# A transformer trunk on one core: the last expert round of each layer in smaller pieces, and what follows it begun on parts

## The reference, cut to what matters

```
for layer in range(2):
    x = x + mixer(rmsnorm(x, norm_mix[layer]))      # layer 0: attention, layer 1: gated linear attention
    x = x + moe(rmsnorm(x, norm_ffn[layer]))        # 32 experts, two of one group for each token
return rmsnorm(x, norm_final)

# moe, for each expert e
hid = silu(h @ w_gate[e]) * (h @ w_up[e])           # 1024 -> 512
y = y + gates[..., e:e + 1] * (hid @ w_down[e])     # 512 -> 1024
```

## Time and profile before

| | us |
|---|---|
| median of three runs | 1184.77 |
| lowest and highest | 1184.62, 1185.75 |
| span of the profiled execution | 1184.7 |
| PE busy in it | 998.1 (84%) |
| DVE, ACT, POOL busy | 276.8, 130.1, 3.5 |

### The profile page before, as it was taken

The page is one execution under the profiler, slowest core; times in us unless marked ns, Lnnn a source line. Parts: engine busy times, 40 slices in busy tenths (PEclk is TensorE's granted clock), DMA queues, the critical chain, the costliest instruction groups (busy, mean ns, idle before and its releaser), DMA issues.

```text
span 1184.7 us, 12720 instructions
## 1 busy us (share of the span) xinstructions
PE 998.1 (84%) x5268; PEld 457.9 (39%) x5268; DVE 276.8 (23%) x653; ACT 130.1 (11%) x309; POOL 3.5 (0%) x10
## 2 busy tenths in 40 slices
PE   8999999967767768977999999999677777779776
PEld 7675553313213213342485555533132132233422
DVE  1265352202102101110322453512011011012103
ACT  2024020000000000000231120200000000000001
POOL 0000000000000000000000000000000000000000
PEclk9999999989879879988999999999898798799889
DMA  9923989999999999999973518999999999999996
GB/s 365 411 77 133 418 329 425 428 427 428 427 430 427 428 429 427 426 426 423 412 327 142 213 71 340 352 428 426 426 430 427 428 429 426 429 427 428 425 422 249
DMA packets 39297, 442.43 MB, mean 373 GB/s; under 512 B 4386, under 2 KB 4770, under 8 KB 12484
## 3 DMA queue, kind: packets, MB, share of 16 engines
q1 hardware_dynamic: 39092, 441.47, 89.4%
q10 hardware_dynamic: 144, 0.13, 0.0%
HBM read 440.54 MB, written 1.05 MB: 373 GB/s over the span
## 4 chain that ended last, share of the span: by engine, by line
PE 52%; DMA 42%; issue 3%; DVE 1%; SPq 1%; ACT 0%; POOL 0%; DVEq 0%; POOLq 0%
PE psum L1707 51%; DMA sb_weights<-moe_w_down 38%; DMA sb_weights<-moe_w_gate 3%; SPq L668 1%; DMA sb_weights<-moe_w_up 1%; DMA sb_weights<-ev_w_in_units 1%; PE psum L2302 0%; DVE sb_weights L1578 0%; DVE sb_x L1598 0%; PE psum L1885 0%; PE psum L1745 0%; PE psum L2170 0%; PE psum L2080 0%; PE psum L1983 0%; ACT sb_weights L914 0%
## 5 line engine op out<-in xcount | busy, mean ns | idle before, releaser
L1707 PE MATMUL psum<-sb_weights,sb_hT 128*32 128x512 f32 (+3 forms) x2368 | 469.4, 629 | 102.9 <-DMA sb_weights<-moe_w_gate 59.8
L1707 PE MATMUL psum<-sb_weights 128*32 128x512 f32 (+12 forms) x1632 | 319.8, 561 | 43.5 <-DMA sb_weights<-moe_w_down 38.7
L1707 PEld LDWEIGHTS psum<-sb_weights,sb_hT 128*32 128x32 f32 (+2 forms) x2368 | 148.2, 128 | 396.0 <-issue 315.7
L1707 PEld LDWEIGHTS psum<-sb_weights 128*32 128x32 f32 (+7 forms) x1632 | 116.2, 139 | 235.2 <-issue 192.1
L1591 DVE TENSOR_TENSOR sb_x<-sb_x,psum 128x512 f32<-128x512 f32 x84 | 57.7, 687 | 281.6 <-PE psum L1707 281.6
L1707 PE MATMUL psum<-sb_hT,sb_weights 128*128 128x256 f32 (+1 forms) x400 | 88.8, 380 | 0.9 <-DMA sb_weights<-ev_w_in_units 0.8
L1707 PEld LDWEIGHTS psum<-sb_hT,sb_weights 128*128 128x128 f32 (+1 forms) x400 | 74.0, 187 | 13.5 <-issue 1.6
L1707 PE MATMUL psum<-sb_weights,sb_hn 128*128 128x192 f32 (+2 forms) x448 | 72.2, 321 | 6.4 <-issue 6.2
L1707 PEld LDWEIGHTS psum<-sb_weights,sb_hn 128*128 128x128 f32 x448 | 69.3, 204 | 11.1 <-issue 11.1
L1583 DVE COPY sb_weights<-psum 96x512 f32<-96x512 f32 (+1 forms) x20 | 13.7, 687 | 180.6 <-PE psum L1707 180.6
L1578 DVE TENSOR_TENSOR sb_weights<-sb_weights,psum 96x512 f32<-96x512 f32 (+1 forms) x22 | 15.0, 684 | 159.5 <-PE psum L1707 159.4
(11 more groups left out here) (201 smaller groups left out, 340.7 us busy)
## 6 DMA issues: line engine op xcount, KB each, us to landing
sb_weights<-moe_w_gate SPq DMA_DIRECT2D x60, 2048.0 KB, 24.5
sb_weights<-moe_w_down SPq DMA_DIRECT2D x58, 2048.0 KB, 27.1
sb_weights<-moe_w_up SPq DMA_DIRECT2D x50, 2048.0 KB, 27.1
sb_weights<-moe_w_up SPq DMA_DIRECT2D x18, 1024.0 KB, 23.2
sb_weights<-od_w_in_units SPq DMA_DIRECT2D x6, 2048.0 KB, 27.4
sb_weights<-ev_w_in_units SPq DMA_DIRECT2D x5, 2048.0 KB, 25.5
sb_weights<-moe_w_up SPq DMA_DIRECT2D x20, 512.0 KB, 8.5
sb_weights<-moe_w_gate SPq DMA_DIRECT2D x16, 512.0 KB, 7.1
```

The lines of the kernel that those rows point to most:

```text
L1707: return nc.tensor.matmul(o, l, r, start=start, stop=stop, skip_group_check=True)
```

## The change

What it does:

- In the last round of each layer the gate matrices too are loaded in two row halves (`last_gate`). PE multiplies the first, scatters both halves of the round before, and multiplies the second; then come three products of 512 columns whose result nobody reads (`keep_warm`), then up as before.
- `LAST_PARTS` becomes four quarters. Quarters 0 and 1 go to the two halves of bank 2, and only after both is ACT told to copy them. The first half is scattered after quarter 1, then the third quarter is multiplied, copied by ACT and scattered, then the fourth is multiplied, and scattered.
- DVE adds the third quarter before it copies the fourth. In layer 1 the means of the squares of the final norm (`mean_by_arrival`) stand between them.
- ACT squares by arrival: halves of both tiles, third quarters, fourth quarters, and the root adds the fourth's sum to the rest.
- The second mixer: the transposes go by pairs of column blocks for both tiles (`turn_blocks`): blocks 0 to 3 before the fourth quarter's scatter, 4 and 5 behind it, 6 and 7 in the middle of the low-rank product. ACT scales the first four blocks, DVE the others, with a mean between and after them. The spread of the inverse moves behind the first half of the first projection.
- The final norm: GpSimd multiplies the first halves of x by the gain when they are complete, ACT scales them by 1/rms, DVE does the second halves as before. y is stored in two DMAs of a whole tile.
- Semaphores of the two mixers are merged, with other counts; no instruction moves by that.

The core of the diff:

```diff
-LAST_PARTS = ((0, 2), (2, 3), (3, 4))
+LAST_PARTS = ((0, 1), (1, 2), (2, 3), (3, 4))
...
-                    if columns and kind == "up":
+                    if columns and kind != "down":
                         for half in range(2):
...
-                                sp.dma_start(unit[SLOT[kind] + k][:, at], src[:, at]).then_inc(last_up[half], 16)
+                                sp.dma_start(unit[SLOT[kind] + k][:, at], src[:, at]
+                                             ).then_inc((last_gate if kind == "gate" else last_up)[half], 16)
...
             for t in range(TILES):
-                for half in range(2):
-                    cols = slice(half * HALF, (half + 1) * HALF)
-                    sp.wait_ge(x_done, 2 * t + half + 1)
-                    sp.dma_start(out[0, t * P:(t + 1) * P, cols], y[:, t, cols]).then_inc(out_stored, 16)
+                sp.wait_ge(final_first, t + 1)
+                sp.wait_ge(final_second, t + 1)
+                sp.dma_start(out[0, t * P:(t + 1) * P, :], y[:, t]).then_inc(out_stored, 16)
...
+            gp.wait_ge(gfin_done, 2)
+            for t in range(TILES):
+                gp.wait_ge(main.x_added, 8 * ROUNDS + t + 1)
+                gp.tensor_tensor(y[:, t, 0:HALF], x[:, t, 0:HALF], gfin[:, 0:HALF], ALU.mult).then_inc(final_weighted, 1)
...
+            def sums_by_arrival(n):
+
+                nc.scalar.activation(warm2, warm, ACT.Sqrt).then_inc(act_chain, 1)
...
+                if n == 2:
+                    for b in range(4):
+                        act.wait_ge(hT_psum, turns(n) + b // 2 + 1)
+                        nc.scalar.activation(hT[:, b], psum[:, b // 2, (b % 2) * SEQ:(b % 2 + 1) * SEQ], ACT.Copy,
+                                             scale=gain[:, n, b:b + 1]).then_inc(hT_first, 1)
+                for part, (first, end) in enumerate(((0, HALF), (HALF, 3 * QUARTER), (3 * QUARTER, D))):
+                    for t in range(TILES):
+                        if part == 1:
+                            act.wait_ge(third_added, TILES * layer + t + 1)
+                        else:
+                            act.wait_ge(main.x_added, base + part + t + 1)
...
+                        nc.scalar.activation(scrap[:, first:end], x[:, t, first:end], ACT.Square, accum_out=total
+                                             ).then_inc(sumsq_done, 1)
+                        if part == 2:
+                            act.wait_ge(ms_done, i + 1)
+                            act.wait_ge(sumsq_done, sums(n) + 2 * TILES + t + 1)
+                            nc.scalar.activation(rms[:, i:i + 1], total, ACT.Sqrt, bias=ms_part[:, i:i + 1], scale=1.0 / D
+                                                 ).then_inc(rms_done, 1)
...
+            def mean_by_arrival(n, t):
...
+                dve.wait_ge(sumsq_done, sums(n) + t + 1)
+                chained(nc.vector.tensor_scalar(part, first, 1.0 / D, EPS, ALU.mult, ALU.add))
+                dve.wait_ge(sumsq_done, sums(n) + TILES + t + 1)
+                nc.vector.scalar_tensor_tensor(out=part, in0=third, scalar=1.0 / D, in1=part, op0=ALU.mult, op1=ALU.add
+                                               ).then_inc(ms_done, 1)
...
                 add_round(s, r + 1, (0, 1))
+                add_last(2, third_scat, 2 * layer, THIRD_BANKS, third_added)
+                if layer:
+                    for t in range(TILES):
+                        mean_by_arrival(4, t)
                 dve.wait_ge(s.used["down"], r + 2)
-                nc.vector.tensor_copy(ysel[0:ROUND_SLOTS, 3 * QUARTER:D], psum[0:ROUND_SLOTS, LAST_BANKS[2], 0:QUARTER]
+                nc.vector.tensor_copy(ysel[0:ROUND_SLOTS, 3 * QUARTER:D], psum[0:ROUND_SLOTS, LAST_BANKS[3], 0:QUARTER]
                                       ).then_inc(s.y1_done, 1)
-                add_last(2, third_scat, 2 * layer, THIRD_BANKS, third_added)
                 add_last(3, s.scat_psum, (r + 1) * 4 + 2, FOURTH_BANKS, s.x_added)
...
-                multiply(0, s.y0_psum)
-                multiply(1, third_psum)
+                multiply(0, None)
+                multiply(1, s.y0_psum)
                 scatter(s, n, h, 0)
-                multiply(2, s.used["down"])
+                multiply(2, third_psum)
                 pe.wait_ge(third_done, k + 1)
                 for t in range(TILES):
                     pe.wait_ge(s.x_added, n * 4 + (t + 5))
                     scatter_quarter(2, THIRD_BANKS, t, third_scat)
+                multiply(3, s.used["down"])
+                if k == 0:
+                    for bank in range(2):
+                        turn_blocks(bank, (2 * bank, 2 * bank + 1), (s.x_added, n * 4 + 5))
                 pe.wait_ge(s.y1_done, n + 1)
                 for t in range(TILES):
+                    if t:
+                        pe.wait_ge(third_added, TILES * k + 1)
                     scatter_quarter(3, FOURTH_BANKS, t, s.scat_psum)
                 if k == 0:
-                    turn_h(1, halves_in(2)[0:2])
+                    turn_blocks(2, (4, 5), (third_added, 1))
```

213 lines of the change are left out of this document (132 added, 81 removed).

## The result

| | us |
|---|---|
| before, median of six runs | 1184.96 (1183.59 to 1185.75) |
| changed, median of six runs | 1189.51 (1186.86 to 1191.27) |
| ratio | 1.0037, 95% interval 1.0027 to 1.0047 |
| profiled execution of the changed kernel: time, span | 1188.12, 1186.3 |

The change makes the kernel 4.5 us slower. Forecast were 1185.8 and "no change" as the likeliest; 1189.5 lies outside the range. In every execution listed with both, the time is 1.8 us above the span.

The account below looks back on a forecast made before the run. DMA bytes were taken to bound the expert rounds, PE the mixers. 1184.7 less 0.2 for the mixer plus 1.2 for the end gave 1185.7, as a median 1185.8; range 1182.0 to 1188.2.

Parts of the forecast that it names:

- Start of the gates, waits, fill-in hidden: Last round: 7 us gate wait goes, PE idles up to 3.9 before the second up half, fill-in products cost nothing.
- T = 1164.9: Start of down products in layer 1's last round: 1163.4 plus 1.5 clock loss, against 1165.83 before.
- finer quarters: Down loads of the last round: with more quarter pieces the last lands 0.3 us later, at 1173.0.
- What is won there stays won: Second mixer: PE-bound, its loads wait for PE, so time won between the layers lasts; gain 0.2 us.
- Open copies: Down quarters of the last round: PE's scatters wait for ACT's two uncovered copies, 0.85 and 0.65 us.
- Means holding the copy: Layer 1's tail: DVE's means wait for ACT's squares and delay the last quarter's copy, 1.5 us of new wait.
- Stores: End of layer 1: the last store is twice as large, +0.6 us on 2.5.
- Tail: Layer 1, from the start of the down products to the end: 21.0 us against 18.9.
- Table load: ACT in layer 1's tail: 1.28 us, without the skill's drain of some 1.38.
- (b): Rival: clock falls and stays down over the down quarters, 1.3 us more at each end; 1188.4, slower, chance 0.2.
- (a): Rival: clock holds through the 3.9 us idle and DVE's means don't hold the copy; 1181.2, faster, chance 0.2.
- (c): Rival: DMA's last quarter comes after PE is ready, so the change doesn't reach the end; 1185.0, forecast with it 0.5.

Follow-up runs that it names:

- The fill-in run: Changed kernel with its three fill-in products moved into the wait between the two up halves: 1186.39, ratio 1.0011.
- all repairs: Changed kernel, gate halves and twelve down loads kept, with fill-in products between the up halves, both ACT copies covered, DVE's copy first: 1185.87, ratio 1.0004.
- gates and fill upon the norm parts: Kernel keeping only the change's second mixer and final norm parts, plus gate halves and fill-in products between the up halves: 1189.05, ratio 1.0034.
- the gates filled: Kernel before, with five fill-in products of 512 columns ahead of PE's wait for the last gates: 1186.30, ratio 1.0007.
- the run with the copies covered: Changed kernel with the third down quarter's product put ahead of the first half's scatter: 1188.27, ratio 1.0029.

## Why the prediction was wrong

Its sum was +1.0 from profile to profile. From A on the two profiles of the change stand 4.4 above the two of before.

*Start of the gates, waits, fill-in hidden:* right in layer 1 of the first profile, each within 0.5 us; in the second the gates waited 1.32 us there, and in layer 0 of the first the wait before the second up half was 2.81, not 3.9. That the early gates would be given back at the second up half was right too.

*"T = 1164.9", and 574.0 in layer 0: this step failed.* It took the landing of the second up half from before and set 5.8 plus a clock loss of 1.5 behind it. The loss was 1.5 to 1.7, near enough. But the landings moved. From A, layer 0's comes after 381.1 and 381.2 in before, 381.7 and 382.6 in the change; in layer 1, counted from the same whole-down issue (776.63, 776.42; 776.37, 777.72), after 381.0, 381.1 and 381.7, 383.0. By the means that is 1.0 and 1.3 later, 2.4 in all against the landings that the sum used, where the text said of the three new issues on SP "nothing", and 0.3 for finer quarters. About 1.1 of it is the longer packets, which the prediction could not see in its rows, and about 0.9 the finer pieces (0.2 MB in the last round of each layer, beyond what the longer packets explain); the rest is within what one execution differs from the next. The cause of the longer packets stays open.

*"What is won there stays won": not in every execution.* The mixer did go on from T as summed (134.19 from D0 to PE's 128x512 group at 707, 134.10 before), so what the second mixer's parts gain only makes up for the later start of its transposes. But in the first profile the gathers at 742 ran at 0.57 of the clock, 3.39 us for 2.00, and with what follows them made the stretch to the next whole downs 1.2 longer (69.43 against 68.26). In the second they took 2.00, and PE waited for a load instead, 0.98 where before waits 0.17 and 0.33, so that the stretch was 0.8 longer:

```profile
751.80 1.92 PE L1789 MATMUL psum<-sb_weights,sb_hT 128*32 128x512 f32 x12 [0.98 <-DMA sb_weights<-moe_w_up]
```

The mixer is thus not bound by PE alone up to its end. Over all profiles D0 to the next whole downs takes 201.4 to 203.6, whatever the kernel, so this term may be chance.

*Open copies* 0.70 and 0.49 for 0.85 and 0.65, and 9.7 from T to the last quarter's product for 9.8: right. *Means holding the copy:* right in kind, 0.6 instead of 1.5. ACT's first squares followed each other at 0.61 where I set 0.81 with the read, and the quarters' at 0.40 for 0.61; they were done at T+12.2, not T+13.0. *Stores:* 3.7 us behind the last product, where I had 3.1. *Tail:* +1.8 for the forecast 2.1. *Table load:* 1.28, and the next square 1.40 after its start, so there is no drain in the rows; the Trainium skill (ScalarE: Activation LUTs, What ACT_TABLE_LOAD costs) has one of 1.38 and does not agree here.

The account, from two profiles of each: 1.0 forecast, +2.4 for the landings, +0.5 from the landings to T (mostly the larger clock losses), +0.9 ahead of layer 1's whole downs, -0.3 for the tail: 4.5, measured 4.4. That it closes says that no segment is forgotten, not that each term is a fixed cost; a landing differs by up to 1.3 from one profile of the changed kernel to the other.

*Rivals.* (b), the clock down over the down quarters, did not happen: 48 records take 3.65, the full rate. Its time, 1188.4, was nearest for the wrong reason. (a) had the clock held and the means off the copy's path. The fill-in run gave the second up half its full clock, the condition that alone was to give 1182.7, and came to 1186.39, 1.3 above before; with the means moved too it came to before's time and not to 1181. The later landings, and the stores that took 0.6 more than forecast, are what (a) had not counted. (c) was set aside too soon: in the change as it is PE is late, but where PE comes earlier it waits for the down loads (1.51 with all repairs, 2.07 with gates and fill upon the norm parts), and in before as well (1.45 in layer 0, 1.25 with the gates filled).

*The measure.* The span was taken for a time. That did no harm to the number, since 1184.7 is near the median by chance and the sum of +1.0 on the median gives 1185.8 too; but it hid that the profile of before was of an execution 1.5 us above the median, and so that 1.6 from profile to profile meant 3.5.

## What to carry to other kernels

Where loads set the pace, ask of every early start what it waits for next: TensorE's loss at the gates cost next to nothing here, because a transfer behind it came no sooner. Fill-in products belong into the last wait ahead of work that is on the path; a loss ahead of a load's wait was free here. A landing can't be taken over from the kernel before when the loads are cut otherwise, and not even when they are the same: compare the mean time of one packet in a stretch that the change doesn't touch. When one engine's list is rearranged, the copy that another engine waits for comes before adds and means, and two profiles are compared from a common instruction behind which the change begins, not from zero.

## What had not been expected

The same wait need not cost the same: 3.86 us idle ahead of the second up half left it at 3.63 us in the run with the copies covered, 3.87 made it 5.33 in the changed kernel, and in layer 0 3.27 left it and 2.81 slowed it. A forecast of what one such wait costs is a chance, not a number. Executions of one kernel lie 4 to 5 us apart (1186.75 to 1191.48 without the fill-in products), once 8 (before, 1183.14 to 1191.29 in 35); how much of that is the clock was not separated.

SP's issue of a load takes 0.33 us, but a median of 2.0 for the twelve down issues of the last round. It was 1.97 for nine in before; new with the gate halves is that the up issues ahead of them stretch too.

```profile
L672 SPq DMA_DIRECT2D sb_weights<-moe_w_down x12: 332/2000/4576, 1136.4 to 1158.6; - x12
```

The Trainium skill (DMA: Bandwidth & Descriptors, Bandwidth) gives a transfer of 1 MB, issued by GpSimd, 341 GB/s, 78% of the peak, and advises at least that size. Here, in a queue that is full, pieces of 1 and 0.5 MB moved 417 GB/s from 1120 to 1160 where before, with part of them 2 MB, moved 422: the size costs about 1%, not 22.

GpSimd's two products of 512 columns took 2.51 us, 1.26 each for the forecast 1.2, and were done 6.7 us ahead of their use.
